# A PEER layer whose second table is multiplied as dense weight matrices for four of eight token tiles

## What is computed

```python
PEER_HEADS, PEER_NKEYS, PEER_TOPK, PEER_CHUNK = 8, 128, 16, 128      # 128 * 128 = 16384 experts
def peer(xn, w_q, sub_keys, u, v):                                   # u, v: (16384, 1024)
    def chunk(xc):                                                   # 128 tokens
        q = (xc @ w_q).reshape(PEER_CHUNK, PEER_HEADS, 2, PEER_DHALF)
        s = jnp.einsum('thzd,znd->thzn', q, sub_keys)
        s1, i1 = lax.top_k(s[:, :, 0], PEER_TOPK)
        s2, i2 = lax.top_k(s[:, :, 1], PEER_TOPK)
        ...                                                          # the best 16 of the 256 pairs
        eidx = jnp.take_along_axis(cidx, pos, axis=-1)               # (t, 8 heads, 16)
        gate = jax.nn.softmax(top, axis=-1)
        act = jax.nn.gelu(jnp.einsum('thkd,td->thk', u[eidx], xc), approximate=False)
        return jnp.einsum('thk,thkd->td', gate * act, v[eidx])
```

## Time and profile before

| | |
|---|---|
| median of the runs | 4022.99 us |
| the profiled execution, its span | 4023.9 us |
| PE, DVE, POOL, ACT busy (share of the span) | 69%, 61%, 53%, 21% |
| bytes moved by DMA | 1422.97 MB, a mean of 354 GB/s |
| of these by POOL's queue (nearly all U and V rows) | 1086.75 MB |
| U fetches, V fetches | 1024, 1024 |

### The profile page before, as it was taken

How to read it: one execution, slowest core, us unless ns; L and a number is a source line. 1 busy time by engine, 2 the same in 40 slices (tenths; PEclk the granted TensorE clock), 3 DMA queues, 4 the chain that set the end, 5 groups by cost and what they waited for, 6 DMA issues and landing times.

```text
span 4023.9 us, 41489 instructions
## 1 busy us (share of the span) xinstructions
PE 2788.8 (69%) x14155; PEld 1429.4 (36%) x14155; DVE 2439.3 (61%) x5186; ACT 858.2 (21%) x2057; POOL 2121.6 (53%) x2149
## 2 busy tenths in 40 slices
PE   6899999898975677796676767455757753333334
PEld 4787777544342322333333323122323320000000
DVE  4552446527676666556766665677766667666652
ACT  4333213402143301112333011132320110000000
POOL 1000205013576656556766565676665667777775
PEclk9999999999987888897887888778888875565566
DMA  8944865567999999999999999999999999999998
GB/s 223 258 154 143 228 209 169 180 240 268 413 407 393 403 410 412 413 412 393 393 400 405 412 400 413 401 406 397 392 406 411 389 409 409 410 408 408 402 409 336
DMA packets 472416, 1422.97 MB, mean 354 GB/s; under 512 B 66152, under 2 KB 136784, under 8 KB 464016
## 3 DMA queue, kind: packets, MB, share of 16 engines
q0 software_dynamic: 298768, 1086.75, 69.5%
q1 hardware_dynamic: 173152, 332.95, 23.2%
q10 hardware_dynamic: 288, 0.62, 0.1%
HBM read 1359.46 MB, written 90.06 MB: 360 GB/s over the span
## 4 chain that ended last, share of the span: by engine, by line
DMA 38%; POOL 13%; PE 9%; issue 8%; DVE 8%; ACT 0%; SPq 0%; DVEq 0%; ACTq 0%; POOLq 0%
DMA ring<-in_peer_u,idx 34%; POOL ring L2459 6%; POOL ring L2452 6%; PE ps_l L1775 5%; DMA ring<-in_peer_v,idxT 4%; DVE ring L2637 4%; PE acc L2683 2%; PE ps_l L1853 1%; PE ps_l L1831 0%; DMA lane<-state_scr 0%; DVE e_f L2560 0%; PE ps_l L1848 0%; DVE hit L2558 0%; DVE where L2520 0%; DVE rest L2521 0%
## 5 line engine op out<-in xcount | busy, mean ns | idle before, releaser
L2637 DVE CUSTOM_DVE_ANT_0 ring<-ring,ps_n2F 128x1024 f32<-128x1024 f32 x1024 | 1242.2, 1220 | 933.3 <-DMA ring<-in_peer_u,idx 922.2
L2459 POOL DMA_INDIRECT ring<-in_peer_u,idx x1024 | 999.1, 976 | 805.8 <-DVE dots L2637 576.3
L2683 PE MATMUL acc<-ring,spread 128*32 128x512 f32 x4096 | 734.7, 853 | 953.3 <-DMA ring<-in_peer_v,idxT 953.1
L2452 POOL DMA_INDIRECT ring<-in_peer_v,idxT x1024 | 993.0, 970 | 336.5 <-issue 297.5
L1775 PE MATMUL ps_l<-lane 128*128 128x512 f32 x1760 | 790.2, 603 | 11.6 <-ACT lane L2100 6.6
L2683 PEld LDWEIGHTS acc<-ring,spread 128*32 128x32 f32 x4096 | 147.7, 136 | 1417.6 <-issue 1415.7
L1775 PEld LDWEIGHTS ps_l<-lane 128*128 128x128 f32 x1760 | 330.8, 193 | 443.8 <-issue 431.4
L562 POOL DMA_DIRECT2D bias<-rpb_scr x16 | 13.2, 829 | 322.5 <-PE ps_dt L846 277.0
L1970 PE MATMUL ps_l<-lane 128*128 128x512 f32 x192 | 117.3, 696 | 56.1 <-DVE nmax L2152 55.8
L2489 ACT ACTIVATE dots<-dots 128x32 f32<-128x32 f32 x32 | 7.3, 229 | 606.1 <-DVE dots L2637 605.9
L2060 ACT ACTIVATE st<-st,nmax 128x512 f32<-128x512 f32 x128 | 92.2, 720 | 184.0 <-DVE nmax L2152 182.9
(11 more groups left out here) (363 smaller groups left out, 4014.7 us busy)
## 6 DMA issues: line engine op xcount, KB each, us to landing
lane<-kept_scr SPq DMA_DIRECT2D x44, 2048.0 KB, 10.6
w_z<-in_w_in SPq DMA_DIRECT2D x16, 1024.0 KB, 6.0
adaB<-in_w_ada SPq DMA_DIRECT2D x16, 1024.0 KB, 6.2
ring<-in_peer_u,idx POOLq DMA_INDIRECT x1024
ring<-in_peer_v,idxT POOLq DMA_INDIRECT x1024, 13.8
kept_scr<-in_w_in SPq DMA_DIRECT2D x6, 2048.0 KB
lane<-w_scr SPq DMA_DIRECT2D x6, 2048.0 KB, 10.9
ada<-in_w_ada SPq DMA_DIRECT2D x8, 1024.0 KB, 15.4
```

Of the source, the lines that this page charges most:

```text
L2452: pool.indirect_dma_start(v_rows[:, nv % RV, :], None, a["peer_v"][0], bass.IndirectOffsetOnAxis(ap=idxT[:, m % 2, col:col + 1], axis=0)). ...
L2459: pool.indirect_dma_start(u_rows[:, n % RU, :], None, a["peer_u"][0], bass.IndirectOffsetOnAxis(ap=idx[:, i % RI, j:j + 1], axis=0)).then_ ...
L2637: nc.vector.tensor_tensor_reduce(out=u_rows[:, n % RU, :], in0=u_rows[:, n % RU, :], in1=ps_n[:, :], scale=1.0, scalar=0.0, op0=ALU.mult, ...
L2683: last = nc.tensor.matmul(acc[q * QUAD:(q + 1) * QUAD, cols], spread[:, m % 2, c0:c0 + QUAD], v_rows[:, nv % RV, cols], start=(g == 0 and ...
```

## The change

Tiles 1 to 4 (DENSE) no longer fetch V rows. For them:

- In `stage_front` SP fills four arrays in memory with zeros, one for each dense tile: 16384 experts by 128 tokens, 8.39 MB each, 33.6 MB in all. The four DMAs stand in SP's program behind the last `load_x` and ahead of the loads and stores of the next part.
- In the loop, DVE works out for each grain of a dense tile the places of its picks in that array (`share_cells`, six operations on 128x32 elements), and POOL issues for each pick an indirect DMA that adds 128 weights of 4 bytes into the array: 512 scatters. They stand 40 slots behind the grain's first slot, 16 in 10 slots and then none in 6; ahead of each 16, POOL waits until the 16 before have landed.
- From slot 762 on SP streams the whole V table in 32 blocks of 2 MB, each with four 256 KB pieces of the arrays, into two buffers. For each block, tile and half of the columns PE multiplies a *unit*: four matmuls of 128x128 by 128x512 (`multiply_block`), and DVE adds it to a total in SBUF (`add_block`). 256 units lie evenly over slots 762 to 1042. Then four whole tiles are scaled, added to h, normed and stored.

V rows are fetched for tiles 0, 5, 6 and 7. Those of tile 0 are spread over slots 45 to 680, one in five slots; those of 5 to 7 stand at the slots at which they stood. RV is 10 instead of 12, h and the weights move into the room set free, and `weigh` of the first grain waits on DVE until that room is free.

```diff
+DENSE = (1, 2, 3, 4)
+KEYS_TOGETHER = 4
+SHARES = NKEYS // KEYS_TOGETHER
+SHARE_FILL = 256
...
+                for scr in share_scr:
+                    rows = scr.rearrange("(p r n) o -> p r (n o)", p=P, n=SHARE_FILL)
+                    sp.dma_start(rows, nothing[:, :].unsqueeze(1).broadcast_to([P, NKEYS * NKEYS // SHARE_FILL, SHARE_FILL])).then_inc(s_filled, 16)
...
-    RU, RV, RI = 6, 12, 2
+    RU, RV, RI, RH = 6, 10, 2, 4
...
+            share_at.setdefault(m * GRAIN + SHARE_AT + k // TOPK * TOPK + k % TOPK * SHARE_PACE // TOPK, []).append((t, j))
...
+        DENSE_FROM, DENSE_TO, DENSE_LAG = PICKS * 6 - 6, PICKS * TT + 18, 2
+        unit_slot = [DENSE_FROM + q * (DENSE_TO - DENSE_FROM) // ALL_BLOCK_UNITS for q in range(ALL_BLOCK_UNITS)]
...
+        def load_shares(sp, c):
+            if c == 0:
+                sp.wait_ge(p_mm, LANE_JOBS)
+            ...
+            if c >= 2:
+                sp.wait_ge(block_mm, (c - 1) * UNITS_A_SHARE)
+            sp.dma_start(v_block[:, c % 2, :, :], v_blocks[c]).then_inc(s_block[c % 2], 16)
+            for i in range(ND):
+                ...
+                sp.dma_start(shares[:, c % 2, i, :], share_scr[i].rearrange("(c b n) o -> c b (n o)", b=NKEYS, n=KEYS_TOGETHER * P)[c]).then_inc(s_part[c % 2], 16)
...
+                        for t, pick in share_at.get(n, ()):
+                            d, g = DENSE.index(t), pick // GRAIN
+                            if pick % GRAIN == 0:
+                                pool.wait_ge(weight_done, GRAINS * t + g + 1)
+                                pool.wait_ge(cell_done, GRAINS * d + g + 1)
+                            if pick and pick % TOPK == 0:
+                                pool.wait_ge(s_share[d], 16 * pick)
+                            pool.indirect_dma_start(share_scr[d], bass.IndirectOffsetOnAxis(ap=cell[:, g % 2, pick % GRAIN:pick % GRAIN + 1], axis=0),
+                                                    weight[:, t % RH, pick:pick + 1], None, compute_op=ALU.add).then_inc(s_share[d], 16)
...
-                    if t:
-                        v.wait_ge(turned_w, m - GRAINS + 1)
+                    ...
+                    elif m == 0:
+                        v.wait_ge(p_mm, SPARE_DONE)
...
+                def add_block(q):
+                    ...
+                    v.wait_ge(block_mm, q + 1)
+                    if c == 0:
+                        nc.vector.tensor_copy(total, bank).then_inc(block_added, 1)
+                    else:
+                        v.wait_ge(block_added, q - UNITS_A_SHARE + 1)
+                        nc.vector.tensor_tensor(total, total, bank, ALU.add).then_inc(block_added, 1)
...
+                def multiply_block(q):
+                    ...
+                    if q >= LANE_BANKS:
+                        pe.wait_ge(block_added, q - LANE_BANKS + 1)
+                    for k in range(KEYS_TOGETHER):
+                        last = nc.tensor.matmul(bank, shares[:, c % 2, i, k * P:(k + 1) * P], v_block[:, c % 2, k, half * HALF:(half + 1) * HALF],
+                                                start=(k == 0), stop=(k == KEYS_TOGETHER - 1))
+                    last.then_inc(block_mm, 1)
```

More of the change, by code:

```diff
@@ L2387, in normed_row, with fetch_slot @@
             return tok[:, [k for k, kind in enumerate(tok_kind) if kind == ("n2", t)][0] % RT, :]
+        SUMMED = [t for t in range(TT) if t not in DENSE]
+        BEFORE = [t for t in SUMMED if t < DENSE[0]]
+        order = {t: i for i, t in enumerate(SUMMED)}
+        v_grain = [GRAINS * t + g for t in SUMMED for g in range(GRAINS)]
+        pace = GRAINS * (DENSE[-1] + 1) / (GRAINS * len(BEFORE))
+        def fetch_slot(s, k):
+            m = v_grain[s]
+            if m < GRAINS * DENSE[0]:
+                return FETCH_AT + int(pace * (s * GRAIN + k))
+            return m * GRAIN + FETCH_AT + k
@@ new lines, in stage_tail @@
+        ended_at = {t: fetch_slot(GRAINS * (order[t] + 1) - 1, GRAIN - 1) for t in SUMMED}
+        fin_at, square_at, root_at, norm_at, out_at, back_at = (
+            {ended_at[t] + after: t for t in SUMMED} for after in (FIN_AT, SQUARE_AT, ROOT_AT, NORM_AT, OUT_AT, BACK_AT))
+        share_at = {}
+        for t in DENSE:
+            for j in range(PICKS):
+                m, k = GRAINS * t + j // GRAIN, j % GRAIN
+                share_at.setdefault(m * GRAIN + SHARE_AT + k // TOPK * TOPK + k % TOPK * SHARE_PACE // TOPK, []).append((t, j))
@@ new lines, in stage_tail @@
+        for c in range(SHARES):
+            block_at.setdefault(unit_slot[(c - 1) * UNITS_A_SHARE] + 1 if c >= 2 else DENSE_FROM - 6 + c, []).append(c)
+        WHOLE_SUM = DENSE_TO + DENSE_LAG + 2
+        RESIDUAL_SLOT, WHOLE_ROOT, WHOLE_NORM = PICKS * (TT - 1) + 8, WHOLE_SUM + 3 * ND + 1, WHOLE_SUM + 3 * ND + 4
+        LANE_JOBS = len(evac_of)
+        LANE_ACTS, LANE_DVES = acts, dves
+        DROOM = KEYS_TOGETHER * DM
+        v_block = lane[:, 0:2 * DROOM].rearrange("p (r a d) -> p r a d", r=2, a=KEYS_TOGETHER)
@@ L2389, in slots @@
         def slots(i):
-            return range(PICKS if i < TT else FIN_SLOT + 16)
+            return range(PICKS if i < TT else END_SLOTS)
         def grain_ended(n, after):
@@ L2440, in _ @@
                         n = i * PICKS + j
-                        m, k = fetched(n)
-                        if m is not None:
+                        for m, k in fetch_at.get(n, ()):
                             nv = m * GRAIN + k
@@ new lines, in add_block @@
+                def add_block(q):
+                    c, i, half = block_unit(q)
+                    total = whole[i][:, half * HALF:(half + 1) * HALF]
+                    bank = ps_l[:, q % LANE_BANKS * HALF:(q % LANE_BANKS + 1) * HALF]
+                    if q == 0:
+                        v.wait_ge(p_mm, LANE_JOBS)
+                        v.wait_ge(p_act, LANE_ACTS)
+                        for k in range(len(st_jobs))[-RS:]:
+                            stored_wait(v, k)
+                    v.wait_ge(block_mm, q + 1)
+                    if c == 0:
+                        nc.vector.tensor_copy(total, bank).then_inc(block_added, 1)
+                    else:
+                        v.wait_ge(block_added, q - UNITS_A_SHARE + 1)
+                        nc.vector.tensor_tensor(total, total, bank, ALU.add).then_inc(block_added, 1)
```

257 lines of the change are left out of this document (177 added, 80 removed).

## The result

| | before | after |
|---|---|---|
| median of the runs | 4023.14 us (4 runs, 4022.44 to 4024.96) | 4510.03 us (4 runs, 4507.17 to 4521.51) |
| ratio after to before | | 1.1213, 95% interval 1.1192 to 1.1233 |
| profiled execution, its span | 4023.9 us | 4519.8 us |
| PE, DVE, POOL busy | 69%, 61%, 53% | 74%, 58%, 54% |
| bytes moved by DMA | 1422.97 MB | 1289.02 MB |

The kernel moves 9% fewer bytes and takes 12% longer. The forecast was 4182 us, with 4060 to 4440 as its range: slower, as expected, but some 330 us beyond the forecast and 70 above the range.

The account below looks back on a forecast made before the run. DMA bounds the loop now, with POOL's issuing and then DVE close behind. Terms: 4023.9 + 36 (front) + 7 - 86 - 154 (scatters) + 0 + 355 (stream) = 4182 us; range 4060 to 4440.

Parts of the forecast that it names:

- What bounds the kernel, slots 168 to 680: Slots 168 to 680: POOL's issuing ends last at 1440 us, DVE's 1113 and DMA hide below; -154 us.
- The price of a scatter: Slots 168 to 680: a scatter costs POOL 1.25 us, gap included, like a 128-entry fetch; bounds 1.07 and 2.18.
- The waits of the grains: Slots 168 to 680: POOL waits about 2 us in each of 16 grains for weights and places from DVE.
- Rival (a): Slots 168 to 680: a scatter costs POOL 1.71 us by three accesses; +82 instead of -154, whole 4418 us; chance 0.18.
- The fixed part of a DMA: Slots 168 to 680: it overlaps for scatters, hidden up to 0.68 us each; otherwise, at 2.0 us each, some 520 more.
- Rival (c): Slots 168 to 680: scatter cheap for POOL, 0.92 us or less; at 0.7 the whole is 3900 us; chance 0.11.
- The stream: Slot 762 to the end: PE (1032 us) and DMA (987) both nearly full; 1105 us with 3% for mutual waits, +355.
- Rival (b): Stream from slot 762: PE keeps falling to its low clock, mean 0.85; +540 us there, whole 4367; chance 0.13.
- Slots 45 to 168: Four of five V fetches go and DVE is next; 300 us with some 4% for surfacing waits, -86 us.
- The front: Before slot 0: a weight load queues behind the zeros on SP and PE waits; +36 us, bounds 0 and +135.
- Slots 0 to 45: New wait on DVE ahead of the first weights, until PE releases POOL; +7 us, bounds 0 and +7.
- 680 to 762: These slots keep the same U and V rows and jobs, no scatter; 0 us, bounds -10 and +10.

## Why the prediction was right or wrong

- **What bounds the kernel, slots 168 to 680: right.** POOL's issue rate is the bound once V fetches go, DVE's work is next, DMA falls to 0.80. All three were seen, though the floor without scatters is 1205 us and not 1113.
- **The price of a scatter: wrong, and this is the step that failed.** "I take 1.25, the row of the same instruction with the same 128 entries." It isn't the same instruction: it adds. The run without the addition measured 0.99 + 0.30 = 1.29, so the row was the right one for a plain scatter, and the addition brings 0.59 more. With the measured mean, 1.61 + 0.30, the forecast's own formula gives 512 x 1.91 + 614 x 1.25 + 32 = 1777, or +183 in place of -154, and the sum becomes 4519; the span was 4519.8. That it comes so near is luck: the errors of the other terms, +16 and -19 the largest, cancel, and so do two within this one, as the next point says. The bounds, 1.07 and 2.18, did hold the price, but the upper one was 4658 us, and the range ended at 4440.
- **The waits of the grains: wrong, without effect.** The forecast has 32 us in this stretch. Ahead of scatters POOL waited under 2 us for DVE; its 22.6 us of waits for DVE stand ahead of U fetches. Against that, a U fetch took 0.98 + 0.30 = 1.28 in the mean where 1.25 was taken.
- **Rival (a) was the case, at more than its price.** "The scatter is dearer" on POOL, by counting accesses, 1.71. It measured 1.88. What spoke against it, "the count of entries is the same", was no reason: the count doesn't tell what POOL does for each. The chance, 0.18, was too low for an operation of which no row showed the essential part. How (a) counts isn't shown: it has 3 accesses to 2, a ratio of 1.5, and measured is 1.58 to 0.99, or 1.6.
- **The fixed part of a DMA.** By the estimates above a scatter takes 0.46 to 0.58 us of the DMA engines, and it stays hidden. The Trainium skill's price of about 2.0 us ("DMA: Bandwidth & Descriptors", section "Anatomy of one DMA") is no cost of occupancy here: the median from issue to landing is 4.6 us and one is issued each 3.5 us of the stretch among U and V fetches, so they overlap, and the 520 us by that page did not come.
- **Rival (c)** needed a scatter at 0.92 or less. Even without the addition it is 1.29, and that kernel, at 4232 (one execution, against 4030), is still slower than before. The forecast's 4182 would have been 50 off for it.
- **The stream: right, for its reason.** 1086 measured for 1105. PE's work was 1051 us (955 + 96) for the forecast's 1032, and it was idle for 35: 6 in the stretch, the end of one wait of 15.3 us for the first pieces, and 28 behind slot 1023. The 3% for two queues that wait on each other did not come. What lies behind slot 1023 is 124 us, since the last units fall there.
- **Rival (b)** fell: the clock is 0.99. As the prediction argued, PE has more work than DMA and does not wait. The rule it was set beside ("TensorE: Matmul & The Clock Gate", section "HAM oscillation" of the Trainium skill) needs such waits. Half of the multiplications bring some back: 128 us of waits for V rows and some 135 for DVE's additions, at a clock of 0.87.
- **Slots 45 to 168**: -70 for -86. Of DVE's 98.8 us of waits for U rows, 9.8 are left, and POOL now waits 145 us for DVE: the bound moved to DVE as said, and 62 us beside its 254 of work remain where 4% were allowed for.
- **The front**: +40 for +36, by the path that the prediction named (the load at SP, the item's weights, PE idle 35.9 us); the last step of it is ACT, which waits for the weights with the emptying of PE's banks behind it. It said nothing of other places for the zeros; three of them cost the same.
- **Slots 0 to 45**: 0, the lower bound; the wait ahead of the first weights has no price. **680 to 762**: 0.

## What to carry to other kernels

An indirect DMA is paid twice, on the engines that carry it and on the queue engine that issues it; when fetches of large rows give way to many tiny transfers, as here, the second price can decide, and bytes say nothing about it. Price it from a row of the very same operation: an option on it (here an addition) that no row shows is an unknown, and its upper bound belongs in the range. Before work is taken off one engine in a stretch, work out every other engine's time for the same stretch, since the gain ends at the next one. A mean share of the DMA engines is not free time: look for it at the place where the new transfers will stand.

## What the runs showed of the hardware

- An indirect DMA that adds in memory kept POOL 1.58 us for 128 entries of 4 bytes, against 0.99 without the addition and 0.96 for a fetch of the same entries; a fetch of 128 rows of 4 KB took 0.94. What POOL does in the additional 0.59 us no run tells.
- By an estimate from share times length it took 0.46 to 0.58 us of the sixteen DMA engines together, against 0.19 without the addition, for 512 bytes. It was 144 packets in POOL's DMA queue, against 32.
- Four DMAs of 8.39 MB from 1 KB a partition repeated held SP's queue for 78.6 us before the next issue. So a store of zeros is not out of the way once it is handed over.
